# Mixture-of-experts rows kept in DRAM tables by indexed transfers, and one preparatory stage folded into the next

## The chip, the cores and the metric

The kernel runs on one core of one Trainium2 chip. The metric is the time of one execution on the device in microseconds (us); smaller is better.

## The reference, cut to what matters

Two transformer blocks run one after the other on 256 tokens of width 1024 in float32. The first block's second layer ends in a mixture of experts: each token goes to 2 of 8 experts. Then come a final norm and the second block, which needs the spectra of its convolution filters and a memory of 256 rows.

```python
def moe_swiglu(h, router, wg, wu, wd):
    logits = (h @ router).astype(jnp.float32)
    top_v, top_i = lax.top_k(logits, TOP_K)
    gates = jax.nn.softmax(top_v, axis=-1)
    combine = jnp.sum(jax.nn.one_hot(top_i, N_EXPERTS, dtype=jnp.float32) * gates[..., None], axis=-2)
    y = jnp.zeros(h.shape, jnp.float32)
    for e in range(N_EXPERTS):
        y = y + combine[..., e:e + 1] * swiglu(h, wg[e], wu[e], wd[e]).astype(jnp.float32)
    return y.astype(h.dtype)

    # end of first_block, then the filters of second_block
    return rmsnorm(x, final_norm)
    ...
    f = jnp.concatenate([fwd, jnp.zeros((1, HY_ORDER, HY_WIDTH), F32), bwd[1:][::-1]], axis=0)
    f = f / (jnp.sum(jnp.abs(f), axis=0, keepdims=True) + EPS)
    return jnp.fft.rfft(f, axis=0)
```

## The kernel before, in words

The kernel is a fixed sequence of stages; a barrier of the compute engines stands between two of them. SP issues nearly all loads. Weights come in slabs of 1 MB into seven slots (`slots`). For float32 accuracy ScalarE copies a slab to a rounded high part (`w_hi`, and in the experts two more buffers `w_hi_more`, L1241), VectorE subtracts to make the low part (`slots_low`, L1293), and TensorE (PE) multiplies three times per slab: high by high, high by low, low by high.

**Router** (after L2612). PE transposes the gained tokens and scores them; VectorE, in steps that each wait for the one before, finds the two experts of each token, its shares and its rank within each expert (L2694 to L2729). `RC` holds for each pass the rank of every token and its share. `jobs` lists the expert of each pass. The stage's PE program ends with `keep_busy(pe, 14, 4)`, 28 matmuls on zeros.

**Experts** (`experts`, L1057). One pass takes up to 128 tokens of one expert; there are 8 passes, or up to 11 when an expert has more tokens. In the profile there are 8. A pass reads 42 slabs in the order of `plan`: seven groups g of four "first" slabs (gate and up) and two "down" slabs, which come one group later. Within a pass:

- `gather` (L1127) makes the input of the next pass: 16 float32 matmuls multiply the token rows `htm` by a 0/1 selection `sel` (made by `choose`, L1262). PE does it just ahead of the last two down slabs. ScalarE and VectorE then split it to `xh`, `xl` (`source`, L1217 and L1268), after `turned_out` of the last group and ahead of their split of the next pass's first slab.
- `empty` (L1223, L1273) copies the sums of the previous pass from PSUM to `y` at the second slab of a pass.
- `scatter` (L1136) brings `y` of the previous pass back to its tokens: four groups of two float32 matmuls by `back`, placed after slabs 2 to 5 of a pass; VectorE adds each to `res` (`add`, L1277). `back` is made from `marks` (selection times share) by two transposes (`turn_marks`, L1154) and a ScalarE copy (L1248).
- `turn` (L1143) transposes the hidden values of a group, four 128x128 blocks.

SP's loop waits for slab i-7 to be used and then issues slab i (L1107). After the last pass SP fetches six slabs of the next part (L340). The last `empty` and four `scatter`, `add` close the stage. SP goes on past the experts' block only when all engines have left it.

**Opening** (`opening`, L1336 on). SP loads the filter's hidden values, the memory `m_tm`, weights and tables (L2753 to L2773). PE sums the squares of `res`, transposes the memory, and keeps busy (`keep_busy(pe, 40, 1)`); VectorE and ScalarE make the root, split the first slab of layer 0 (`split_hi`, `split_lo`), copy the memory to `memT`, and scale `res` in eight tiles.

**Spectra** (`spectra`, L1441 on). PE first waits for all those loads. Four units i run as a pipeline: PE `make` (L1463), VectorE `window` (L1507), GpSimd clears one row, VectorE `mix` (L1514), PE `transform` (L1477), ScalarE copies the even part, VectorE `join` (L1522), and ScalarE's queue stores the 1 MB result to DRAM. At the start of each unit's `transform` PE does `keep_busy(pe, 8, 4)`. The stage ends when ScalarE has seen all four stores land. Layer 0 of the second block follows.

## Time and profile before

| | us |
|---|---|
| median of 3 runs | 2967.62 (2963.11 to 2969.07) |
| span of the profiled execution, from its first to its last instruction | 2947.1 |
| median of the runs less that span | 20.5 |

The profiled execution's time outside its span is not recorded apart; the runs' median stands 20.5 us above the span, and that is taken for what lies around it. In the profile's rows PE is TensorE's matmuls, PEld its weight loads, DVE VectorE, ACT ScalarE, POOL GpSimd, SPq and ACTq the DMA issues of SyncE and ScalarE. A bracket at the end of a timeline row is the idle time before it and what ended it.

### The profile page before, as it was taken

The page shows a single profiled execution, that of the slowest core. Times are in us where ns is not written, and L with a number is a line of the kernel's source. Part 1 is how long each engine was busy: PE and PEld are TensorE (multiplying, and loading weights), DVE is VectorE, ACT ScalarE, POOL GpSimd, SP SyncE. Part 2 cuts the span into 40 slices and gives each one's busy share as a digit, 9 for nine tenths or more (in the row PEclk, how much of TensorE's full clock was granted, in tenths as well). Part 3 has the DMA queues.
Part 4 walks back from the last instruction along what each step waited for, and adds up shares of the span by engine and source line. Part 5 has one row for each costly group of instructions (what it writes and reads, how often), then busy time and mean ns, then how long its engine had stood idle before and what let it go on. Part 6 is the DMA issues. An engine that isn't in the chain of part 4 may idle for free. (4 is left out here: it accounts for less than half of the span.)

```text
span 2947.1 us, 44951 instructions
## 1 busy us (share of the span) xinstructions
PE 2833.8 (96%) x18499; PEld 2512.2 (85%) x18499; DVE 1999.5 (68%) x1985; ACT 1505.3 (51%) x1445; POOL 66.0 (2%) x56
## 2 busy tenths in 40 slices
PE   7999999899999999999999999999999899999999
PEld 6899998788888888888886778999899788999898
DVE  6555565588888888888885656566555665666554
ACT  3544463476666667666663426444434236444442
POOL 1000000000000000000000210000000100000000
PEclk9999999899999999999999999999999999999999
DMA  6255540699999999999996333454365343444453
GB/s 191 77 188 194 173 158 4 234 367 328 347 347 336 356 329 364 327 350 345 331 361 208 134 103 101 145 171 144 101 199 187 122 128 102 149 140 140 133 190 107
DMA packets 365129, 619.48 MB, mean 210 GB/s; under 512 B 14664, under 2 KB 201126, under 8 KB 363700
## 3 DMA queue, kind: packets, MB, share of 16 engines
q1 hardware_dynamic: 363432, 611.77, 60.8%
q10 hardware_dynamic: 1550, 5.57, 0.5%
q8 instruction: 114, 1.87, 0.3%
q14 instruction: 33, 0.27, 0.0%
HBM read 611.93 MB, written 5.37 MB: 209 GB/s over the span
## 5 line engine op out<-in xcount | busy, mean ns | idle before, releaser
L366 DVE TENSOR_TENSOR slots_low<-slots,w_hi 128x2048 fp32r<-128x2048 f32 x240 | 550.2, 2296 | 372.8 <-ACT w_hi L355 372.5
L355 ACT ACTIVATE w_hi<-slots 128x2048 fp32r<-128x2048 f32 x240 | 452.8, 1891 | 324.7 <-PE ps L949 168.5
L1293 DVE TENSOR_TENSOR slots_low<-slots,w_hi 128x2048 fp32r<-128x2048 f32 x224 | 504.2, 2286 | 68.9 <-ACT w_hi L1241 68.9
L468 PE MATMUL ps<-x_hi,w_hi 128*128 128x256 f32 x1520 | 435.7, 287 | 31.8 <-DVE x_lo_low L553 15.7
L468 PE MATMUL ps<-x_lo_low,w_hi 128*128 128x256 f32 x1520 | 428.9, 282 | 0.0
L468 PE MATMUL ps<-x_hi,slots_low 128*128 128x256 f32 x1520 | 428.7, 282 | 0.0
L1241 ACT ACTIVATE w_hi<-slots 128x2048 fp32r<-128x2048 f32 x224 | 416.9, 1908 | 0.9 <-DMA slots<-in_moe_w_up_dram 0.8
L1173 PE MATMUL ps<-slots_low,x_hi 128*128 128x512 f32 x896 | 352.7, 394 | 0.0
L468 PEld LDWEIGHTS ps<-x_hi,w_hi 128*128 128x128 f32 x1520 | 291.6, 192 | 38.8 <-issue 30.4
L468 PEld LDWEIGHTS ps<-x_lo_low,w_hi 128*128 128x128 f32 x1520 | 291.4, 192 | 0.3
L468 PEld LDWEIGHTS ps<-x_hi,slots_low 128*128 128x128 f32 x1520 | 291.6, 192 | 0.0
L949 PE MATMUL ps<-x_hi,w_hi 128*128 128x256 f32 x960 | 268.2, 279 | 1.0 <-DVE x_lo_low L1015 1.0
L949 PE MATMUL ps<-x_lo_low,w_hi 128*128 128x256 f32 x960 | 266.4, 277 | 0.0
L949 PE MATMUL ps<-x_hi,slots_low 128*128 128x256 f32 x960 | 266.2, 277 | 0.0
L1293 DVE TENSOR_TENSOR slots_low<-slots,w_hi_more 128x2048 fp32r<-128x2048 f32 x112 | 255.2, 2284 | 11.0 <-ACT w_hi_more L1241 11.0
L1173 PE MATMUL ps<-w_hi,x_hi 128*128 128x512 f32 x512 | 206.5, 403 | 12.6 <-DVE slots_low L1293 12.6
L1241 ACT ACTIVATE w_hi_more<-slots 128x2048 fp32r<-128x2048 f32 x112 | 208.7, 1919 | 0.0
L1173 PE MATMUL ps<-w_hi,x_lo_low 128*128 128x512 f32 x512 | 202.1, 395 | 0.0
L1173 PEld LDWEIGHTS ps<-slots_low,x_hi 128*128 128x128 f32 x896 | 169.4, 189 | 36.6
L1232 ACT ACTIVATE hidden_hi<-ps 128x512 fp32r<-128x512 f32 x56 | 33.6, 599 | 293.4 <-PE ps L1143 258.8
L949 PEld LDWEIGHTS ps<-x_hi,w_hi 128*128 128x128 f32 x960 | 180.7, 188 | 2.3 <-issue 1.8
L949 PEld LDWEIGHTS ps<-x_lo_low,w_hi 128*128 128x128 f32 x960 | 180.5, 188 | 0.6
(519 smaller groups left out, 5522.0 us busy)
## 6 DMA issues: line engine op xcount, KB each, us to landing
slots<-in_moe_w_gate_dram SPq DMA_DIRECT2D x112, 1024.0 KB, 5.1
slots<-in_moe_w_up_dram SPq DMA_DIRECT2D x112, 1024.0 KB, 5.1
slots<-in_moe_w_down_dram SPq DMA_DIRECT2D x112, 1024.0 KB, 4.9
slots<-in_mlp_w_dram SPq DMA_DIRECT2D x64, 1024.0 KB, 5.3
slots<-in_w_in_dram SPq DMA_DIRECT2D x54, 1024.0 KB, 5.3
slots<-in_ffn_w_gate_dram SPq DMA_DIRECT2D x14, 1024.0 KB, 5.0
slots<-in_ffn_w_up_dram SPq DMA_DIRECT2D x14, 1024.0 KB, 5.0
slots<-in_ffn_w_down_dram SPq DMA_DIRECT2D x14, 1024.0 KB, 4.9
```

Of the source, the lines that this page charges most:

```text
L355: act.activation(w_hi[:, s.buffer, 0:s.kt * s.cols], slots[:, s.slot, 0:s.kt * s.cols], ACT.Copy).then_inc(w_hi_done, 1)
L366: dve.tensor_tensor(slots_low[:, s.slot, 0:n], slots[:, s.slot, 0:n], w_hi[:, s.buffer, 0:n].bitcast(F32), ALU.subtract).then_inc(w_lo_don ...
L468: mm = pe.matmul(b[:, t * T:(t + 1) * T], w, xx[:, k, :], **flags)
L949: mm = pe.matmul(first_bank(g, n)[:, t * T:(t + 1) * T], ww[:, k, t * P:(t + 1) * P], xx[:, k, :], start=(k == 0 and q == 0), stop=(k == K ...
L1173: mm = pe.matmul(b, xx[:, kx, :], ww[:, k, :], start=(kx == 0 and t == 0), stop=(kx == KD - 1 and t == 2))
L1232: act.activation(hth[:, :], bank(TURN), ACT.Copy).then_inc(turned_hi, 1)
L1241: act.activation(his[i % R], raw[i % NS], ACT.Copy).then_inc(hi_done, 1)
L1293: dve.tensor_tensor(low[i % NS], raw[i % NS], his[i % R].bitcast(F32), ALU.subtract).then_inc(lo_done, 1)
```

## The change

The tables `x_rows` and `y_rows` (12 blocks of 128 rows of 4 KB each) are new in DRAM. The router's stage computes for every token its two places in them (`places`) and no longer the share by pass. SP fills 11 blocks of `x_rows` and 3 of `y_rows` with zeros during the router's first stage. At the start of the experts GpSimd sends every token row to its two places by four indirect transfers of 128 rows. In a pass, right after slab 12, SP stores `y` of the previous pass to `y_rows` and loads the next pass's rows to `xr`; `turn_rows`, eight transposes, takes the place of `gather`, which stays for the first pass. `scatter`, `add`, `marks` and their waits leave the passes. After the last pass SP stores the last `y`, GpSimd waits for it and fetches each token's two rows by four indirect transfers, ScalarE and VectorE weigh and join them, PE transposes, and VectorE adds to `res`.

The `opening` stage is gone: its squares, root, memory transposes, scaling and first split stand inside `spectra`. PE there waits for the first seven loads only (`early`); the others are waited for at the end (`late`). `keep_busy` in `transform` is gone; the wait for the stores moves into layer 0 (a hook of ScalarE). The router's last `keep_busy` is 8 instead of 14.

```diff
+        x_rows, y_rows = (nc.dram_tensor(n, (NJOB, P, D), F32).ap() for n in ("expert_rows_in", "expert_rows_out"))
@@ experts, SP's pass
                             sp.wait_ge(used, SLABS * j + i + 1)
+                            if i == 30:
+                                sp.wait_ge(stored, 16 * j + 16)
...
+                            if i == 12:
+                                sp.wait_ge(rows_sent, 16 * 2 * TT)
+                                sp.wait_ge(act_out, j + 1)
+                                sp.wait_ge(dve_out, j + 1)
+                                sp.dma_start(block_of_rows(y_rows, j), y[:, :]).then_inc(stored, 16)
+                                sp.dma_start(xr[:, :], block_of_rows(x_rows, j + 1)).then_inc(rows_in, 16)
@@ after the passes
                         fetch(sp, after + s)
+                    sp.wait_ge(act_out, n + 1)
+                    sp.wait_ge(dve_out, n + 1)
+                    sp.dma_start(block_of_rows(y_rows, n), y[:, :]).then_inc(stored, 16)
+
+                @block.gpsimd
+                def _(pool):
+                    pool.wait_ge(blanked, 32)
+                    for t in range(TT):
+                        for k in range(2):
+                            pool.indirect_dma_start(x_flat, bass.IndirectOffsetOnAxis(ap=places[:, 0, k, t:t + 1], axis=0), htm[:, t, :], None).then_inc(rows_sent, 16)
+                    n = pool.value_load(jobs[0:1, NJOB:NJOB + 1], min_val=NE, max_val=NJOB - 1)
+                    pool.wait_ge(stored, 16 * n + 16)
+                    pool.tensor_tensor(all_stored[:, :], number[:, 0:1], number[:, 0:1], ALU.add).then_inc(rows_kept, 1)
+                    pool.wait_ge(rows_kept, 1)
+                    for t in range(TT):
+                        for k in range(2):
+                            pool.indirect_dma_start(back[:, t, k, :], None, y_flat, bass.IndirectOffsetOnAxis(ap=places[:, 1, k, t:t + 1], axis=0)).then_inc(back_in[t], 16)
@@ experts, PE
-                    def scatter(j, g):
-                        pe.wait_ge(added, 4 * j + g + 1)
-                        for m in range(2):
-                            f = (2 * g + m) * P
-                            mm = pe.matmul(bank(MISC)[:, m * T:(m + 1) * T], y[:, f:f + P], back[:, :], start=True, stop=True)
-                        mm.then_inc(scattered, 1)
+                    def turn_rows(j):
+                        pe.wait_ge(rows_in, 16 * j + 16)
+                        for half in range(2):
+                            b = bank((GATE, UP)[half][1])
+                            for k in range(4 * half, 4 * half + 4):
+                                mm = pe.transpose(b[:, k % 4 * P:(k % 4 + 1) * P], xr[:, k * P:(k + 1) * P], eye[:, :])
+                            mm.then_inc(gathered, 1)
-                                if (g, n) == (2, 1):
-                                    turn_marks()
-                                if (g, n) in ((0, 3), (1, 0), (1, 1)):
-                                    scatter(j, {(0, 3): 1, (1, 0): 2, (1, 1): 3}[g, n])
                                 if g == G - 1 and n == 0:
-                                    pe.wait_ge(chosen, j + 2)
-                                    gather()
+                                    turn_rows(j)
                     n = passes(pe, body)
-                    for g in range(4):
-                        scatter(n, g)
+                    for t in range(TT):
+                        pe.wait_ge(joined, t + 1)
+                        for k in range(KD):
+                            mm = pe.transpose(bank(2 + k // 2)[:, k % 2 * T + t * P:k % 2 * T + (t + 1) * P], back[:, t, 0, k * P:(k + 1) * P], eye[:, :])
@@ experts, ScalarE and VectorE after the passes
+                        act.activation(back[:, t, 0, :], back[:, t, 0, :], ACT.Copy, scale=gg[:, t, 2:3]).then_inc(weighed, 1)
+                        dve.scalar_tensor_tensor(out=back[:, t, 0, :], in0=back[:, t, 1, :], scalar=gg[:, t, 3:4], in1=back[:, t, 0, :],
+                                                 op0=ALU.mult, op1=ALU.add).then_inc(joined, 1)
-                        add(n, g)
+                        dve.tensor_tensor(flat(res[:, 2 * g:2 * g + 2, :]), flat(res[:, 2 * g:2 * g + 2, :]), bank(2 + g), ALU.add)
@@ router
+                    nc.sync.dma_start(x_rows.rearrange("a p n -> p a n")[:, 1:NJOB, :], blank[:, :].unsqueeze(1).broadcast_to([P, NJOB - 1, D])).then_inc(blanked, 16)
+                    nc.sync.dma_start(y_rows.rearrange("a p n -> p a n")[:, NE + 1:NJOB, :], blank[:, :].unsqueeze(1).broadcast_to([P, NJOB - 1 - NE, D])).then_inc(blanked, 16)
-                            keep_busy(pe, 14, 4)
+                            keep_busy(pe, 8, 4)
@@ spectra, PE
-                                keep_busy(pe, 8, 4)
+                                else:
+                                    pe.wait_ge(memory_act_out, 2)
+                                    pe.wait_ge(memory_dve_out, 2)
-                        pe.wait_ge(*needs)
+                        mean_squares()
+                        pe.wait_ge(*early)
                         make(0)
+                        turn_memory()
@@ spectra, VectorE
                         window(0)
                         mix(0)
+                        for g in (1, 3):
+                            dve.wait_ge(memory_turned, g + 1)
+                            dve.tensor_copy(flat(memT[:, 2 * g:2 * g + 2, :]), bank(4 + g)).then_inc(memory_dve_out, 1)
+                        dve.reciprocal(ms[:, :], ms[:, :]).then_inc(root_inverted, 1)
                         for i in range(N):
                             if i + 1 < N:
                                 window(i + 1)
+                            else:
+                                split_lo(dve, BEFORE_MOE, len(stream.slabs))
...
                             join(i, 1)
+                            scale_tiles(range(3 * i, min(3 * i + 3, KD)))
@@ spectra, ScalarE
-                        act.wait_ge(spectra_out, 16 * N)
```

## Rows read from the trace of the kernel before

**Rows 1.** The page's first line.
```profile
span 2947.1 us, 44951 instructions
```
**Rows 2.** Busy time by stretch: one pass, the opening, the spectra.
```profile
core 0: us, PE busy (x) PEld busy (x) DVE busy (x) ACT busy (x) POOL busy (x), PEclk, DMA share, GB/s
810.90:939.00 128.10, 127.46 (x582) 104.33 (x582) 107.39 (x68) 88.18 (x64) 0.00 (x0) 1.00 0.96 343
...
1587.50:1608.60 21.10, 17.98 (x125) 15.27 (x125) 8.68 (x13) 6.48 (x7) 1.46 (x2) 0.84 0.70 204
1608.60:1658.00 49.40, 46.57 (x220) 29.00 (x220) 30.13 (x46) 12.79 (x16) 11.54 (x8) 0.97 0.27 107
```
**Rows 3.** Waits in six passes, 690 to 1446 us: total, times, longest.
```profile
PEld ps L1173 <- DVE slots_low L1293: 5.6, 5, 1.1
```
**Rows 4.** DMA, 540 to 560 us, in 40 slices; last column issue to landing.
```profile
GB/s 0 0 0 0 0 53 111 254 389 406 401 414 406 410 397 393 393 377 389 389 389 389 385 381 385 393 385 385 385 389 389 393 406 365 365 393 397 393 385 381
...
slots<-in_moe_w_gate_dram SPq DMA_DIRECT2D x4, 1024.0 KB, 10.9
```
**Rows 5.** DMA, 690 to 1446 us: packets, MB, share; issues to landing.
```profile
q1 hardware_dynamic: 109972, 261.12, 96.5%
...
slots<-in_moe_w_gate_dram SPq DMA_DIRECT2D x83, 1024.0 KB, 5.1
```
**Rows 6.** DMA issues of the whole span: KB each, median us to landing.
```profile
m_tm<-in_mem_dram SPq DMA_DIRECT2D x1, 1024.0 KB, 5.6
...
out_dram<-rows_out ACTq DMA_DIRECT2D x2, 512.0 KB, 2.7
```
**Rows 7.** Timeline of a pass's end and the next one's start.
```profile
797.47 0.59 PEld L1143 LDWEIGHTS ps<-eye,hidden 128*128 128x128 f32 x4
...
800.70 3.77 PEld L1127 LDWEIGHTS ps<-select,by_token 128*128 128x128 f32 x32
...
804.40 0.30 PEld L1195 LDWEIGHTS ps<-w_hi_more,hidden_hi 128*128 128x128 f32 x2
...
806.62 3.72 ACT L1241 ACTIVATE w_hi<-slots 128x2048 fp32r<-128x2048 f32 x2
...
808.56 4.49 DVE L1293 TENSOR_TENSOR slots_low<-slots,w_hi 128x2048 fp32r<-128x2048 f32 x2 [2.53 <-ACT w_hi L1241]
...
810.91 0.19 PEld L1173 LDWEIGHTS ps<-w_hi,x_hi 128*128 128x128 f32 x1 [1.11 <-DVE slots_low L1293]
...
819.05 0.86 PEld L1136 LDWEIGHTS ps<-select_back,y 128*128 128x128 f32 x4
...
819.93 0.19 PEld L1173 LDWEIGHTS ps<-w_hi,x_hi 128*128 128x128 f32 x1
```
**Rows 8.** Line L1154: ns min/median/max, first and last start.
```profile
L1154 PEld LDWEIGHTS ps<-eye,share_marks x16: 140/142/142, 589.5 to 1486.4; 128*128 128x128 f32 x16
```
**Rows 9.** Timeline from the router's end to the first expert load.
```profile
531.02 6.02 PE L630 MATMUL ps<-zeros 128*128 128x256 bf16 x28
...
533.03 0.16 DVE L2729 CAST passes<-passes_f 1x13 int32<-1x13 f32 x1
...
541.67 1.04 SPq L1107 DMA_DIRECT2D slots<-in_moe_w_gate_dram  x2
```
**Rows 10.** Timeline of the experts' end.
```profile
1579.06 0.60 ACT L1223 ACTIVATE y<-ps 128x512 f32<-128x512 f32 x1 [5.05 <-PE ps L1195]
...
1586.76 0.69 DVE L1277 TENSOR_TENSOR res<-res,ps 128x512 f32<-128x512 f32 x1 [1.22 <-PE ps L1136]
1587.72 0.53 SPq L2753 DMA_DIRECT2D filter_hidden<-filter_hidden  x1
```
**Rows 11.** Timeline of the opening's end and the spectra's start.
```profile
1602.11 1.75 DVE L1373 RECIPROCAL mean_square<-mean_square 128x256 f32<-128x256 f32 x1
...
1608.59 7.11 PE L1463 MATMUL ps<-hy_w,filter_hidden 65*128 65x512 f32 x16 [0.97 <-PEq L181]
...
1615.54 1.91 PE L630 MATMUL ps<-zeros 128*128 128x256 bf16 x16
```

More of the change, by code:

```diff
@@ L1057, in experts @@
         def experts(gate, up, down, routed, after):
-            RC, htm, jobs, row_number, number, before, over = routed
+            rank, htm, jobs, row_number, number, before, over, gg, places = routed
             W, G, NS, R, KH = 512, 7, 7, 6, 4
@@ L1295, in body @@
                                 empty(j)
-                            if (kind, g) == ("first", 1):
-                                add(j, n)
                             if (kind, n) == ("first", 0) and g >= 1:
@@ L1439, in sine_layers, with spectra @@
             return {("act", 0): tables, ("pe", 0): first, ("dve", 1): angle(0), ("act", 2): sine(0), ("pe", 2): second, ("dve", 3): angle(1), ("act", 4): store}
-        def spectra(h2, w3s, needs):
+        def spectra(h2, w3s, tiles, m_tm, early, late):
+            gain = gain_of("final_norm", 0)
             dft = K["dft"][:, :].rearrange("p (t s k) -> p t s k", t=TT, s=2)
@@ L1445, in spectra @@
             with ExitStack() as c:
-                fb = sb(c, "filters", [P, 2, TT, 512])
-                pq = [sb(c, "combined", [P, 2, TT, 512]) for _ in range(2)]
-                ab = sb(c, "sizes", [P, 2, TT, 512])
-                F = sb(c, "spectra", [P, 4, 512])
+                fb, pq, ab, ms = tiles
+                F = m_tm[:, :, :].rearrange("p t (a n) -> p (t a) n", n=512)
                 evens = flat(x_lo_plain[:, 0:4, :]).rearrange("p (s n) -> p s n", s=2)
@@ L1452, in spectra, with mean_squares, turn_memory @@
                 N = len(U)
-                with stage("made", "windowed", "lag0", "mixed", "absd", "added", "summed", "sized", "inverted", "transformed", "evens_out", "joined") as \
-                        (block, made, windowed, lag0, mixed, absd, added, summed, sized, inverted, transformed, evens_out, joined):
+                sq = x_hi_plain
+                with stage("made", "windowed", "lag0", "mixed", "absd", "added", "summed", "sized", "inverted", "transformed", "evens_out", "joined",
+                           "ones_row", "squared", "means_made", "shifted", "rooted", "root_inverted", "scaled", "memory_turned", "memory_act_out", "memory_dve_out") as \
+                        (block, made, windowed, lag0, mixed, absd, added, summed, sized, inverted, transformed, evens_out, joined,
+                         ones_row, squared, means_made, shifted, rooted, root_inverted, scaled, memory_turned, memory_act_out, memory_dve_out):
                     @block.tensor
                     def _(pe):
+                        def mean_squares():
+                            for h in range(2):
+                                pe.wait_ge(squared, h + 1)
+                                for k in range(4 * h, 4 * h + 4):
+                                    mm = pe.matmul(bank(7)[:, 0:T], ones[:, :], sq[:, k, :], start=(k == 0), stop=(k == KD - 1))
+                            mm.then_inc(means_made, 1)
+                        def turn_memory():
+                            pe.wait_ge(memory_in, 16)
+                            for g in range(KD // 2):
+                                if g == 3:
+                                    pe.wait_ge(shifted, 1)
+                                for kk in range(2):
+                                    for t in range(TT):
+                                        k = 2 * g + kk
+                                        mm = pe.transpose(bank(4 + g)[:, kk * T + t * P:kk * T + (t + 1) * P], m_tm[:, t, k * P:(k + 1) * P], eye[:, :])
+                                mm.then_inc(memory_turned, 1)
                         def make(i):
@@ L1499, in _, with scale_tiles @@
                     def _(dve):
+                        def scale_tiles(tiles):
+                            for k in tiles:
+                                dve.scalar_tensor_tensor(out=res[:, k, :], in0=res[:, k, :], scalar=gain(k), in1=ms[:, :], op0=ALU.mult, op1=ALU.mult).then_inc(scaled, 1)
                         def window(i):
@@ L2740, in program @@
                 by_row = [A[n][0].rearrange("e (k p) n -> p e k n", p=P) for n in ("moe_w_gate", "moe_w_up", "moe_w_down")]
-                experts(*by_row, (RC, htm, jobs, row_number, number, before, over), BEFORE_MOE)
+                experts(*by_row, (rank, htm, jobs, row_number, number, before, over, gg, places), BEFORE_MOE)
         memT = sb(ctx, "memory", [P, KD, T])
@@ L2776, in program @@
                 fetch(sp, i)
-            with stage("cleared_") as (block, cleared_):
-                @block.gpsimd
-                def _(pool):
-                    pool.memset(wlr_all[:, :, :, :], 0.0).then_inc(cleared, 1)
-                    pool.memset(h2[64:65, :, :], 1.0)
-            opening(m_tm)
-            cm.close()
-            spectra(h2, w3s, (spectra_in, 16 * loads))
+            spectra(h2, w3s, (fb, pq, ab, ms), m_tm, early, (tables_in, 16 * loads))
         for l in range(2):
```

199 lines of the change are left out of this document (88 added, 111 removed).

## The prediction

> **What bounds the kernel now.** I read the page first, for the span [rows 1], then the busy time by stretch. In a pass of the experts PE is busy 127.46 of 128.10 us, VectorE 107.39, ScalarE 88.18, and the DMA engines show a share of 0.96 [rows 2]. A pass lasts 128.1 us by a line that runs once in each: (1486.4 - 589.5) / 7 [rows 8]. So eight passes hold a third of the time, and the question is which of two full resources sets their pace. Two views decide it. In the waits of six passes PE stands still for VectorE's low part five times, 1.1 us each [rows 3], and for nothing else. And a slab lands 5.1 us after its issue in these six passes [rows 5]; at the start, when six or more slabs are queued, it takes 10.9 [rows 4]. In the passes no queue builds up: SP issues a slab when PE has freed a slot, and the DMA follows. So PE's own instructions set the pace, and what is taken off PE in a pass shortens it, as far as the DMA and VectorE can follow.
>
> **The change part by part, in a pass.** Scatter goes: its four matmul instructions hold the weight-load queue from 819.05 to 819.93, 0.88 us, four times a pass [rows 7]: 3.5 us. The two transposes of the marks go: at 0.59 / 4 = 0.15 each [rows 7] 0.3 us. Gather held it from 800.70 to 804.40, 3.70 us [rows 7]; eight transposes at 0.15 take its place, 1.2 us, so 2.5 us less. Not all of that arrives. The stall of 1.11 us at the next pass's first matmul hangs on a chain: gather, ScalarE's two copies, its split of the next first slab at 806.62, VectorE's low part at 808.56 [rows 7]. With the transposes both copies are ready as soon as ScalarE has the last group's hidden values; I place the split 2.3 us earlier, so the pass gains 2.3 and the stall grows a little. Together 3.5 + 0.3 + 2.3 = 6.1 us. The scatters also gave VectorE time: slabs 2 to 5 each had 0.88 us more. In slabs 4 to 7 I follow PE at 2.75 us a slab and VectorE at 4.49 / 2 = 2.25 [rows 7] with its two other operations, and find margins of 0.1 to 0.5 us; four adds of 0.69 [rows 10] leave VectorE too. I take 0.5 off: **5.6 us a pass**, 122.5 us. VectorE has then some 104.6 us of work in 122.5.
>
> What is added to a pass is on the DMA: 0.5 MB stored and 0.5 MB loaded behind slab 12, one slab more than 42. SP's waits there ask for copies made at the pass's second slab, and its wait at slab 30 is for a store issued eighteen slabs before; behind them stand only loads that are not yet due. 43 slabs are 45.1 MB; in 122.5 us that is 368 GB/s. With a queue standing the trace shows 377 to 397 GB/s in most half microseconds and 385 or 389 in the steady ones [rows 4]; at 389 the 45.1 MB take 116 us. So I cost the added rows at nothing: they come when five loaded slabs wait in the slots, and a landing of 5.1 us may grow by 2.7 there. If that cover were gone, they would cost 2.7 us a pass. The bounds for the seven later passes are a gain of 2 us each (the DMA rival below) and 6.1 each.
>
> The Trainium skill, SBUF — State Buffer, section "A bandwidth-pool intuition that's wrong (but worth ruling out)", gives HBM to one core as about 358 GB/s and calls HBM almost always the end-to-end bottleneck. The trace shows more, 385 to 389 GB/s held with a queue. By the page's figure a pass would take 126 us, an estimate, and the whole some 2952 us.
>
> Seven passes: 7 x 5.6 = **39.2 us less**.
>
> **First pass.** The same 5.6 us less, but GpSimd's four indirect transfers write 2 MB about when the first slabs load, with a queue standing [rows 4]. At 389 GB/s that is 5.4 us of DMA time. Between 0 (all done before the first load) and 5.4 I take 2.5, since they can begin some 3 us before the first load. **3.1 us less.**
>
> **Router.** Its end is PE's keep-busy: 28 matmuls of 6.02 us from 531.02, to 537.0; VectorE has finished at 533.2 [rows 9]. Sixteen take 3.4 us: 2.6 us less. VectorE loses eight small steps and gets twelve, at 0.2 us each (its last one took 0.16 [rows 9]), and ends near 534.0, still before. `pick_more` loses three steps of 0.25, and SP's first load at 541.67 [rows 9] waits for it: 0.7 us. The blank rows are 14 stores of 0.5 MB, 7.3 MB, 19 us at 389 GB/s, issued near 514 on an idle DMA; done near 534, ahead of the first load. **3.3 us less**; nothing, if they run late.
>
> **End of the experts.** This grows. Before, from `y` copied (1579.06 + 0.60) to the last add (1586.76 + 0.69) it took 7.8 us [rows 10]. After: the store of `y`, as the 512 KB of the output, 2.7 [rows 6], and 0.2 to hand over; GpSimd's small add 0.5; four indirect transfers; ScalarE's weighing, two of its 0.60 copies, 1.2; VectorE's join, two of 0.69, 1.4; eight transposes at twice 0.15 after the pause, 2.4; four adds, 2.8. No row shows an indirect transfer. Below: four overlapped 512 KB moves, 2.7 + 3 x 1.35 = 6.7. Above: one after another, each as the 1 MB memory load, 5.6 [rows 6], 22.4. I take 9, near the lower end, as they move 4 KB rows like the output's store, with 2.3 more for GpSimd to make 512 addresses. Sum 20.2, so **12.4 us more** (10 to 26).
>
> The Trainium skill, DMA: Bandwidth & Descriptors, section "Anatomy of one DMA — SWDGE (gpsimd) path", fits such a transfer as 2.0 us plus the bytes at 436 GB/s: 3.2 us for 512 KB, an estimate. One after another they would take 12.8 us in place of my 9, and the whole 2932 us. No row here shows one.
>
> SP's next loads began at 1587.72, 0.3 us after the last add, though SP had been idle [rows 10]: they wait for the block's end and move with it.
>
> **Opening and spectra.** Before, the first spectra matmul starts 1608.59 - 1587.72 = 20.9 us after the first load's issue [rows 10, 11]. The DMA engines are busy 0.70 x 21.1 = 14.8 us there for 4.3 MB [rows 2]; the seven early loads and the memory are 3.3 MB of it, 11.3 us, and with some 2.7 for the first to land [rows 6] PE can start at 14: 6.9 us earlier. PE has paused before, so I let the first unit's matmuls, 7.11 / 2 = 3.55 us [rows 11], run half their time at half clock: 1.8 back. VectorE's reciprocal, 1.75 [rows 11], and two copies of 0.69 now stand ahead of the second window: 3.1 back. That leaves 2.0. The keep-busy of 1.91 us [rows 11] goes from three units in which PE is the pace (busy 46.57 of 49.40 [rows 2]); VectorE gets 1.2 us of scaling in each and I count 1.4 for each unit, 4.3. The split of layer 0's first slab takes the place of a window in the last unit, where VectorE waits for a store. **6.3 us less** (0 to 11).
>
> **The sum.** -39.2 - 3.1 - 3.3 + 12.4 - 6.3 = -39.5 us. The profiled span of 2947.1 [rows 1] becomes 2908; the runs' median, 20.5 us above it, becomes **2928 us**. Two of the six high buffers move in memory, as the tiles ahead of them change size; I cost that at nothing, and allow 1 us a pass either way.
>
> **The rivals.** (a) The DMA sets the pass. For it: share 0.96 now at 261.12 MB in 756 us, 345 GB/s; divided by the 96.5% of [rows 5] that is 358 GB/s, so 45.1 MB need 126 us, 2 us less a pass and not 5.6. Against it: landings stay at 5.1 us. Time: 3.5 x 7 = 25 us of the gain is lost, 2952. The page's 358 is the same case. (b) VectorE's low part becomes late in every group. For it: the thin margins above. Against: 104.6 of 122.5 us. At 0.4 us for each of seven groups, 2.8 us a pass, 22 over all: 2950. (c) Slower than before: GpSimd's indirect transfers are slow because it makes 128 row addresses for each. Place: the experts' end, where all engines wait. With t for one, the end costs 4t in place of 9. The gain of 39.5 is gone at t = 12.1 us, 95 ns a row; at 16 us the time is 2983. From about that point the rows sent ahead of the first pass are late for SP's wait at slab 12 as well. For it: nothing on GpSimd in the trace tells its price. Against: each row is 4 KB, and 128 are few.
>
> **How the numbers follow.** The forecast 0.60, with its own range 2915 to 2941; (a) 0.13; (b) 0.10; (c), any indirect transfer over 6 us, 0.17, of which 0.06 stays faster. A change within 0.2%, 6 us, can't be told from none. Faster 0.60 + 0.13 + 0.10 + 0.06 = 0.89, rounded to 0.88; same 0.05; slower 0.07. The range for 8 in 10 goes from 2913, where the bounds fall well together (passes 6.1, the first one undisturbed, the end 10, the spectra 11: 14 us), to 2954, which takes in (a) and (b).
>
> **What would show it.** Passes of 122 to 123 us with PE as busy as now and slabs landing in under 8 us: the main term. Landings that grow to 10 us and more, with PE waiting on low parts that wait on loads: (a). Waits of PE on VectorE of 0.3 us or more in each group at usual landings: (b). At the experts' end: last matmul to next loads about 21 us; more than 30 is (c). First spectra matmul about 14 us after the loads' start, units of 9 and not 10.4 us. The prediction is wrong above all if the passes stay over 126 us.

## The result, and the profile after

The changed kernel takes 2917.35 us (median of 4 runs, 2916.47 to 2919.49), the kernel before on the same chip 2965.86 (4 runs, 2963.11 to 2969.07): 0.9848 of it, 95% interval 0.9822 to 0.9874. The prediction was 2928, range 2913 to 2954, faster.

Every later listing gives an execution's own time beside its span; the time is the span and 1.75 to 1.9 us (once 2.3). The profile of before was thus one of some 2949 us, and the 20.5 us between the runs' median and the span of [rows 1] do not lie around the span. By the profiles the change is worth 31 us, by the runs 48. Profiled and timed executions of the kernel before differ in TensorE's mean granted clock: 0.987 in the profile, 0.979 to 0.984 in most timed ones (below, first experiment). So stages are compared by profile, whole kernels by runs. One run of `spectra_busy` below, 3509.96 us at a mean clock of 0.742, is left out of its median.

The page's first line of the changed kernel, the busy time of one pass (columns as in [rows 2]), the waits and the DMA of six passes, and the line that stores a pass's result, which runs once in each pass:

```profile
span 2915.9 us, 43813 instructions
```
```profile
904.20:1026.00 121.80, 121.01 (x542) 98.32 (x541) 104.05 (x60) 87.86 (x62) 0.00 (x0) 1.00 1.01 371
```
```profile
PE ps L1217 <- DVE hidden_lo L1305: 4.9, 6, 1.0
...
PEld ps L1200 <- DVE slots_low L1311: 1.9, 6, 0.3
```
```profile
slots<-in_moe_w_up_dram SPq DMA_DIRECT2D x86, 1024.0 KB, 5.3
...
expert_rows_out<-y SPq DMA_DIRECT2D x6, 512.0 KB, 6.7
next_rows<-expert_rows_in SPq DMA_DIRECT2D x6, 512.0 KB, 7.4
```
```profile
L1124 SPq DMA_DIRECT2D expert_rows_out<-y x8: 367/368/1081, 575.2 to 1428.1; - x8
```

A pass lasts (1428.1 - 575.2) / 7 = 121.8 us where it lasted 128.1 [rows 8]. PE is as busy in it as before [rows 2], the stall on the low part that was 1.1 us in five of six passes [rows 3] is 0.3, and the wait has gone to the last group's hidden values, 4.9 / 6 = 0.8 us. Slabs land in 5.3 us; right behind the added rows, at slab 13, a landing takes 8.6 us (median of six passes), and it is back at 5.2 by slab 30.

The end of the experts, the counterpart of [rows 10], from the timeline:

```profile
1531.92 0.60 ACT L1245 ACTIVATE y<-ps 128x512 f32<-128x512 f32 x1 [5.77 <-PE ps L1217]
...
1532.83 0.36 SPq L1134 DMA_DIRECT2D expert_rows_out<-y  x1
1535.67 0.19 POOL L1144 TENSOR_TENSOR all_stored<-number 128x1 f32<-128x1 f32 x1 [991.29 <-DMA expert_rows_out<-y]
1536.14 0.98 POOL L1148 DMA_INDIRECT rows_back<-expert_rows_out,places  x1 [0.27 <-POOL all_stored L1144]
1537.42 0.95 POOL L1148 DMA_INDIRECT rows_back<-expert_rows_out,places  x1 [0.30 <-issue]
...
1542.91 1.15 ACT L1277 ACTIVATE rows_back<-rows_back,shares 128x1024 f32<-128x1024 f32 x1 [10.39 <-DMA rows_back<-expert_rows_out,places]
...
1545.46 1.15 ACT L1277 ACTIVATE rows_back<-rows_back,shares 128x1024 f32<-128x1024 f32 x1 [1.40 <-DMA rows_back<-expert_rows_out,places]
...
1549.99 2.48 DVE L1345 TENSOR_TENSOR res<-res,ps 128x512 f32<-128x512 f32 x4 [2.06 <-PE ps L1232]
1552.73 0.53 SPq L2784 DMA_DIRECT2D filter_hidden<-filter_hidden  x1
```

The store of `y` takes 2.8 us, GpSimd hands over an indirect transfer every 1.25 us, and the second pair has landed 9.3 us after the first transfer was issued (1536.14 to 1545.46).

The spectra stage in tens of us, the changed kernel first, then the kernel of the first experiment that has this change's experts and the old opening and spectra (clock: third number from the end):

```profile
1566.60:1576.60 10.00, 10.00 (x23) 5.76 (x24) 4.25 (x6) 0.83 (x2) 0.52 (x1) 0.50 0.15 56
1576.60:1586.60 10.00, 10.00 (x38) 5.74 (x37) 9.97 (x13) 4.16 (x6) 2.87 (x2) 0.97 0.01 2
1586.60:1596.60 10.00, 10.00 (x21) 4.17 (x19) 8.58 (x13) 2.49 (x4) 3.03 (x2) 0.66 0.55 210
```
```profile
1575.30:1585.30 10.00, 10.00 (x36) 5.28 (x37) 7.62 (x10) 2.25 (x3) 2.95 (x2) 1.00 0.00 0
1585.30:1595.30 10.00, 10.00 (x49) 6.19 (x48) 7.31 (x11) 2.95 (x4) 3.38 (x3) 1.00 0.26 107
1595.30:1605.30 10.00, 10.00 (x49) 6.19 (x48) 7.31 (x11) 3.20 (x4) 2.87 (x2) 1.00 0.55 210
```

PE is busy throughout in both, but in the changed kernel it runs at 1.2 GHz, half clock, in all of the first stretch and in two thirds of the third (0.50 and 0.66). The first unit's eight matmuls take 7.19 us where 16 took 7.11 before [rows 11], after PE has waited 5.94 us for loads, and the memory's transposes take 3.62:

```profile
1566.58 7.19 PE L1439 MATMUL ps<-hy_w,filter_hidden 65*128 65x512 f32 x8 [5.94 <-DMA dft<-in_c_dft_dram]
...
1573.57 3.62 PE L1430 MATMUL ps<-eye,m_tm 128*128 128x128 f32 x16
```

And VectorE's scaling, beside GpSimd's add, in the same stage:

```profile
1587.42 3.35 DVE L1484 SCALAR_TENSOR_TENSOR res<-res,vectors,mean_square 128x256 f32<-128x256 f32 x3
...
1587.98 2.52 POOL L1550 TENSOR_TENSOR sizes<-sizes 128x1024 f32<-128x1024 f32 x1 [4.56 <-ACT sizes L1560]
...
1590.70 0.15 DVE L1536 TENSOR_SCALAR filter_size<-ps 128x4 f32<-128x4 f32 x1
...
1590.92 0.50 PEld L1455 LDWEIGHTS ps<-combined,dft 128*128 128x128 f32 x2 [1.38 <-issue]
```

The three tiles take 3.35 us. The line's own durations (shortest, median, longest, in ns) say how:

```profile
L1484 DVE SCALAR_TENSOR_TENSOR res<-res,vectors,mean_square x8: 467/474/2617, 1587.4 to 1610.2; 128x256 f32<-128x256 f32 x8
```

A tile takes 0.47 us, but the one that comes up while GpSimd adds ends only after the add, and takes 2.6 us. The filter's size (L1536) stands behind it, and PE's next transform behind the size.

Stage by stage, in us of the two profiles:

| stretch | before | after | difference | predicted |
|---|---|---|---|---|
| start to the router's squares (same code) | 512.9 | 515.6 | +2.7 | 0 |
| router, to the first expert load | 28.8 | 27.0 | -1.8 | -3.3 |
| first load to the experts' last matmul | 1037.3 | 989.3 | -48.0 | -42.3 |
| to the spectra's loads | 8.8 | 20.8 | +12.1 | +12.4 |
| to the first spectra matmul | 20.9 | 13.9 | -7.0 | -6.9 |
| to layer 0's first matmul | 50.6 | 56.0 | +5.4 | +0.6 |
| to the end (same code) | 1287.9 | 1293.3 | +5.4 | 0 |

The stages that the change touches sum to -39.3 us. The two that it does not touch add 8.1; over the 14 profiles of this study the first of them takes 512.9 to 526.7 us, the last 1283.6 to 1293.4.

### The profile page after: what moved, and what is told of

It is laid out like the page before. It is cut to its first block and busy times, and to the rows that moved or that the text cites. A ratio compares the mean times of both kernels' runs of the same rounds, so it can differ in the third digit from the quotient of the medians.

```text
span 2915.9 us, 43813 instructions
## 1 busy us (share of the span) xinstructions
PE 2779.7 (95%) x17995; PEld 2459.6 (84%) x17995; DVE 1980.1 (68%) x1922; ACT 1506.8 (52%) x1439; POOL 75.1 (3%) x66
## 5 line engine op out<-in xcount | busy, mean ns | idle before, releaser
L471 PE MATMUL ps<-x_hi_low,w_hi 128*128 128x256 f32 x1520 | 435.9, 287 | 32.9 <-DVE x_lo_low L556 15.3
L471 PE MATMUL ps<-x_hi_low,slots_low 128*128 128x256 f32 x1520 | 428.8, 282 | 0.0
L1200 PE MATMUL ps<-slots_low,x_hi_low 128*128 128x512 f32 x896 | 351.6, 392 | 0.0
L471 PEld LDWEIGHTS ps<-x_hi_low,w_hi 128*128 128x128 f32 x1520 | 292.6, 192 | 39.9 <-issue 30.6
L471 PEld LDWEIGHTS ps<-x_hi_low,slots_low 128*128 128x128 f32 x1520 | 292.8, 193 | 0.0
L952 PE MATMUL ps<-x_hi_low,w_hi 128*128 128x256 f32 x960 | 269.0, 280 | 1.0 <-DVE x_lo_low L1018 1.0
L952 PE MATMUL ps<-x_hi_low,slots_low 128*128 128x256 f32 x960 | 267.0, 278 | 0.0
L1200 PE MATMUL ps<-w_hi,x_hi_low 128*128 128x512 f32 x512 | 203.7, 398 | 9.1 <-DVE slots_low L1311 9.1
L1200 PEld LDWEIGHTS ps<-slots_low,x_hi_low 128*128 128x128 f32 x896 | 168.9, 189 | 36.9
L952 PEld LDWEIGHTS ps<-x_hi_low,w_hi 128*128 128x128 f32 x960 | 180.6, 188 | 2.3 <-issue 1.8
L952 PEld LDWEIGHTS ps<-x_hi_low,slots_low 128*128 128x128 f32 x960 | 181.4, 189 | 0.0
```

The lines of the kernel that those rows point to most:

```text
L471: mm = pe.matmul(b[:, t * T:(t + 1) * T], w, xx[:, k, :], **flags)
L952: mm = pe.matmul(first_bank(g, n)[:, t * T:(t + 1) * T], ww[:, k, t * P:(t + 1) * P], xx[:, k, :], start=(k == 0 and q == 0), stop=(k == K ...
L1200: mm = pe.matmul(b, xx[:, kx, :], ww[:, k, :], start=(kx == 0 and t == 0), stop=(kx == KD - 1 and t == 2))
```

## The experiments

Each ran beside the kernel before; a ratio is to that. They ran on four chips, on which the kernel before took 2955.8 to 2965.8 us (medians), so times of two rows compare to some us only. Medians of 5 runs unless said.

**The two parts apart, and the kernel before once more.** `experts_only` is before with the tables alone, `spectra_only` before with the merged opening and spectra alone; `before_again` is before.

> The experts by tables alone; opening, memory's transposes and spectra stage as before. Theory: this part carries the whole gain. By the two traces the passes gave 48.0 us (6.4 a pass and 3.2 in the first), the router 1.8, and the experts' end took 12.0 back: 37.8 us less, about 2928 us against 2966 of before. Rival: the merged spectra stage is worth ten us or more of the 48.5 that the runs differ by; then this kernel stays above 2932. In the profile: passes of 121.7 to 122 us, last matmul of the experts to next loads 20 to 21 us, loads to first spectra matmul 20.9 us as before.

> The merge of opening and spectra alone; experts as before. Theory: the first spectra matmul comes 7 us earlier after the loads and the stretch from it to layer 0's first matmul takes 56 us where it took 50.6, so 1.6 us less in all: 2964 against 2966, not to be told from no change. Rival: it is worth the 10 us that the runs leave beside the experts' part: 2956.

> The kernel before, unchanged, for a second profile. Its first profiled execution took 2949 us, its timed runs 2958 to 2971, while the profiles of every other kernel lie within 10 us of their timed runs. Theory: the first profile caught an execution with a quick first block (its router stage began at 512.9 us; the others' at 515.6 to 521.5, with the same code up to there), and a second profile will show a span of 2955 to 2970 with the excess before the router stage or in the two last layers, not in the experts. Rival: profiled executions of this kernel are always some 17 us quicker than timed ones; then this one shows 2945 to 2950 again.

| kernel | runs, us | ratio (95%) | passes | last matmul to loads | to spectra | to layer 0 |
|---|---|---|---|---|---|---|
| `experts_only` | 2919.30 | 0.9852 (0.9829 to 0.9875) | 121.8 | 21.4 | 20.6 | 50.4 |
| `spectra_only` (6 runs) | 2951.85 | 0.9954 (0.9938 to 0.9970) | 127.9 | 11.4 | 15.0 | 56.2 |
| `before_again` (11 runs) | 2966.57 | 1.0022 (1.0005 to 1.0039) | 128.1 | 8.8 | 21.1 | 50.4 |

The kernel before, run against itself, comes out at 1.0022 with an interval that leaves out 1: differences of some 0.2%, 6 us, are not to be read.

The experts' tables alone give the changed kernel's time within its interval; on top of them the merge takes another 2 us off, nothing that the runs can tell. They come out 9 us under their forecast of 2928. Alone on the kernel before, the merge measured 14 us less where 2 were forecast, though its own stretches, from the experts' last matmul to layer 0, are 2.2 us longer than before's in the profiles: by their rows it gains nothing, and where the 14 us are stays open. The two parts' gains, 46 and 14 us, are not additive either: the whole measured 48.5. The second profile of before is again of an execution at a high clock:

```profile
core 0: 2944.4 us, clock 0.986
```

Of the 57 runs of before in these experiments, the 11 at a mean clock of 0.986 to 0.988 took 2945 to 2958 us, the 45 at 0.979 to 0.984 took 2958 to 2977 (one at 0.985: 2956). So the theory of a second profile at 2955 us and more fell, and the 17 us go with the clock. That is a correlation: no profile of the kernel before at 0.98 was caught, so in which stage the 17 us lie stays open. The rival on record, that a profiled execution of this kernel is always quicker, is not excluded: both profiles are of quick ones, and one run in five is.

**Terms of the pass, put back.** Two kernels restore PE's old work in the passes of the changed kernel, `scatter_back` and `gather_back`; a third, `rows_4mb`, adds DMA. Their edits, in that order:

```diff
+    def scatter(g):
+        for m in range(2):
+            f = (2 * g + m) * P
+            pe.matmul(bank(MISC)[:, m * T:(m + 1) * T], y[:, f:f + P], htm[:, 0, 0:T], start=True, stop=True)
...
+    if g == 0 and n == 2:
+        pe.wait_ge(act_out, j + 1)
+        pe.wait_ge(dve_out, j + 1)
+        scatter(0)
+    if (g, n) in ((0, 3), (1, 0), (1, 1)):
+        scatter({(0, 3): 1, (1, 0): 2, (1, 1): 3}[g, n])
```
```diff
-    turn_rows(j)
+    pe.wait_ge(rows_in, 16 * j + 16)
+    gather()
```
```diff
+    EXTRA = (13, 16, 19, 22, 28, 31, 34)
...
+    if i in EXTRA:
+        m = EXTRA.index(i)
...
+        sp.dma_start(back[:, m % 4 // 2, m % 2, :], block_of_rows(x_rows, j + 1)).then_inc(extra_in[m], 16)
```

> The changed kernel with the scatter's matmul instructions put back into each pass, two at each of slabs 2 to 5, their results left unused and no adds behind them. Theory: PE sets the pass, so the four times 0.88 us of the prediction come back, 3.5 us: passes of 125.2 us where there are 121.7, some 28 us over eight passes. Rival: VectorE or the DMA sets the pass by now; then there is slack for them on PE and the passes stay under 123.

> The changed kernel with the old gather's sixteen matmul instructions at the end of each pass in place of the eight transposes; they fetch pass 0's rows every time, so every pass computes on those. Theory: the end of the pass hangs on the chain of gather, copies and the next first slab's split, so 2.3 us come back, up to the 2.5 that gather takes longer: passes of 124.0 to 124.3 us. Rival: the chain has slack and the passes stay under 122.5; then the gain of 6.4 a pass came from the scatter and VectorE's adds.

> The changed kernel with seven more loads of 0.5 MB in each pass (the next pass's rows again, to where nothing reads them before the experts' end): 45.1 + 3.7 = 48.8 MB a pass. Theory: PE sets the pass and the DMA has the rate that a standing queue showed, 385 to 389 GB/s, so the pass grows only to 48.8 MB / 389 = 125.4 us, 3.7 more, with landings that no longer fall back to 5 us: about 30 us in all. Rival: at 45.1 MB in 121.7 us, 370 GB/s, the DMA is at its end already; then the passes take 131.9 us and the run 80 us more. If it can do more than 389, the passes stay under 124.

The store's line in each, once a pass, in that order:

```profile
L1124 SPq DMA_DIRECT2D expert_rows_out<-y x8: 367/368/393, 578.8 to 1455.2; - x8
```
```profile
L1124 SPq DMA_DIRECT2D expert_rows_out<-y x8: 367/368/1177, 577.9 to 1447.5; - x8
```
```profile
L1129 SPq DMA_DIRECT2D expert_rows_out<-y x8: 368/368/903, 576.9 to 1450.6; - x8
```

Passes of 125.2, 124.2 and 124.8 us against 121.8; by their one run each the kernels take 2944.69, 2937.61 and 2937.35 us. The scatter costs 3.4 us (predicted 3.5), gather 2.4 in place of the transposes (2.3), so PE's instructions set the pass. The marks' two transposes (0.3 by their rows) were not put back. With 3.7 MB more a pass grows by 3.0 us, where the DMA, if it were at its end at 370 GB/s would have made it 131.9. The DMA and the waits of six passes of `rows_4mb`:

```profile
DMA packets 117633, 288.93 MB, mean 393 GB/s; under 512 B 4844, under 2 KB 4844, under 8 KB 117631
...
slots<-in_moe_w_gate_dram SPq DMA_DIRECT2D x84, 1024.0 KB, 11.7
```
```profile
ACT w_hi_more L1273 <- DMA slots<-in_moe_w_gate_dram: 53.0, 46, 2.0
```

Landings stay at 12 us, ScalarE waits for slabs, and 393 GB/s is what the DMA gives here. The changed kernel's 371 GB/s is near that: by this estimate the DMA would set the pass once some 121.8 x (1 - 371 / 393) = 6.8 us more were taken off PE.

**What the experts' end costs.** The indirect fetches are replaced by plain loads on SP's queue.

```diff
-    pool.indirect_dma_start(back[:, t, k, :], None, y_flat, bass.IndirectOffsetOnAxis(ap=places[:, 1, k, t:t + 1], axis=0)).then_inc(back_in[t], 16)
+    sp.dma_start(back[:, t, k, :], y_rows[2 * t + k]).then_inc(back_in[t], 16)
```

GpSimd's small add ahead of its transfers goes with them.

> The changed kernel with the experts' results fetched by four plain loads of 512 KB on SP's queue in place of GpSimd's four indirect ones; they fetch the first four tables as they stand, so tokens get rows that are not theirs. It prices the indirection. The four indirect transfers took 9.3 us from the first issue to the first weighing, of which GpSimd's own steps of 1.25 us are 5. Theory: the transfer of 2 MB sets most of it, 5.4 us at 389 GB/s and some 2 us for the first to land, so plain loads save 1.5 to 2.5 us, and last matmul to next loads falls from 20.8 to 18.5. Rival: the making of addresses sets it; then plain loads take 4 us less and the end 16 to 17 us.

```profile
1542.72 1.77 SPq L1138 DMA_DIRECT2D rows_back<-expert_rows_out  x4
1547.56 1.15 ACT L1274 ACTIVATE rows_back<-rows_back,shares 128x1024 f32<-128x1024 f32 x1 [7.89 <-DMA rows_back<-expert_rows_out]
...
1551.25 1.15 ACT L1274 ACTIVATE rows_back<-rows_back,shares 128x1024 f32<-128x1024 f32 x1 [2.54 <-DMA rows_back<-expert_rows_out]
```

The last pair lands 8.5 us after the first issue in place of 9.3, and last matmul to next loads takes 19.5 us; it takes 20.8 in the changed kernel and 21.1 to 21.6 in five others with indirect fetches and no added loads. The indirection, GpSimd's small add included, is worth 1 to 2 us; the rest is 2 MB on their way and the chain behind them.

**What the merged spectra stage loses.** `scale_moved` moves the scaling, `spectra_busy` puts keep-busy matmuls back.

```diff
     window(i + 1)
...
+    if i:
+        scale_tiles(range(3 * i - 3, min(3 * i, KD)))
     join(i, 0)
...
     join(i, 1)
-    scale_tiles(range(3 * i, min(3 * i + 3, KD)))
```
```diff
     mean_squares()
+    keep_busy(pe, 20, 4)
     pe.wait_ge(*early)
...
     if s == t == 0:
...
+        keep_busy(pe, 8, 4)
```

> The changed kernel, with the scaling of res three, three and two tiles at a time behind the window products of units 1 to 3, and the size added up right behind the joins. Theory: in the changed kernel the scaling stalls while GpSimd adds the sizes (3.35 and 3.40 us for three tiles that take 1.2 alone) and PE waits behind it for the size. Away from that add, three tiles take 1.2 to 1.3 us, the transforms of units 1 and 2 begin 1 and 2 us earlier, and the stretch from the first spectra matmul to layer 0's first matmul falls from 56.0 to about 52.5 us; the run comes out 3 to 4 us under the changed kernel's 2917. Rival: the units are paced by matmuls at half clock; then the stretch stays at 55 to 56 us whatever VectorE does.

> The changed kernel with keep-busy matmuls in the spectra stage: twenty pairs while PE waits for the loads, and the old eight pairs ahead of each unit's first transform. Theory: what the merge lost lies in the granted clock. With the old keep-busy work it was 1.00 for the first thirty us of the spectra (0.50, 0.97 and 0.66 in those of the changed kernel); with it back the first unit's eight matmuls take 3.6 and not 7.2 us, the transposes 1.9 and not 3.6, units 1 and 3 transform in 3.6 and not 5.3; against it stand 1.9 us for each unit, half of it in waits that PE has there anyway. From the first spectra matmul to layer 0's first: 56.0 falls to 47 to 50, the run to about 2909. Rival: the scaling behind GpSimd's adds sets the units and the clock is a symptom of PE's waits; then the stretch stays at 56 or grows by the 1.9 us of some units.

`scale_moved`: 2911.75 us, ratio 0.9821 (0.9802 to 0.9840). Of its timeline:

```profile
1595.54 2.34 POOL L1551 TENSOR_TENSOR sizes<-sizes 128x1024 f32<-128x1024 f32 x1 [3.75 <-ACT sizes L1561]
...
1599.32 6.09 PE L1455 MATMUL ps<-combined,dft 128*128 128x512 f32 x8
...
1600.17 1.27 DVE L1484 SCALAR_TENSOR_TENSOR res<-res,vectors,mean_square 128x256 f32<-128x256 f32 x3
```

Three tiles take 1.27 us alone, and no tile of this kernel more than 0.48:

```profile
L1484 DVE SCALAR_TENSOR_TENSOR res<-res,vectors,mean_square x8: 472/476/479, 1600.2 to 1622.8; 128x256 f32<-128x256 f32 x8
```

That the scaling waits for the add is shown. What it costs the stage is not: the stretch to layer 0 came to 54.6 us where 52.5 was forecast, and the five kernels with unaltered spectra code (the changed kernel, `scatter_back`, `gather_back`, `rows_4mb`, `plain_tail`) take 54.2 to 56.6. The transform of unit 1, 5.29 us in the changed kernel, took 6.09 here at half clock, and the matmuls before it 6.33 in place of 5.47, so part of what the move gave went to the clock. The profiled execution, 2922.95 us, is the slowest of this kernel's five.

`spectra_busy`: 2920.02 us, ratio 0.9863 (0.9834 to 0.9892); the stretch grew to 60.9 us where 47 to 50 was forecast. Its clock in tens of us, its first unit's matmuls and one of its keep-busy groups:

```profile
1573.00:1583.00 10.00, 10.00 (x49) 6.07 (x48) 8.63 (x11) 3.08 (x4) 2.86 (x2) 1.00 0.06 19
1583.00:1593.00 10.00, 10.00 (x32) 5.23 (x31) 10.00 (x15) 3.20 (x4) 2.98 (x2) 0.78 0.26 106
1593.00:1603.00 10.00, 10.00 (x41) 5.93 (x39) 5.20 (x8) 1.19 (x2) 0.52 (x1) 0.71 0.29 105
```
```profile
1572.05 3.71 PE L1439 MATMUL ps<-hy_w,filter_hidden 65*128 65x512 f32 x8 [1.99 <-DMA dft<-in_c_dft_dram]
...
1593.79 3.62 PE L633 MATMUL ps<-zeros 128*128 128x256 bf16 x16
```

The first unit is cured: its eight matmuls take 3.71 us, not 7.19. The keep-busy work inside the units did not hold the clock, and it stands on the path: it waits for the size too, behind the scaling, and 1.9 us become 3.6 at half clock. So here keep-busy work cured the unit behind PE's wait for loads, and cost time ahead of the transforms.

**Taking the experts' end back.** The spectra's loads need nothing of the experts' result. `early_loads` issues them inside the experts' end, to space that is free there; `combined` adds the moved scaling, loads ahead of the last six slabs, window products ahead of the mean square on VectorE, and keep-busy matmuls on PE where it waits for rows. In all three PE sums the squares of `res` behind the first unit's matmuls and no longer ahead of them. `combined_2` loads the transform table and the first weights ahead of the first pass. The edit of `combined`, where part 0 is the transform table, the first filter weights and the hidden values, part 1 the window, part 2 the memory and the second filter weights (in `early_loads` part 0 stands behind the six fetches):

```diff
     n = passes(sp, body)
+    ahead(sp, 0)
     for s in range(AHEAD):
...
     sp.dma_start(block_of_rows(y_rows, n), y[:, :]).then_inc(stored, 16)
+    sp.wait_ge(stored, 16 * n + 16)
+    ahead(sp, 1)
+    for t in range(TT):
+        sp.wait_ge(back_in[t], 32)
+    ahead(sp, 2)
...
     pe.wait_ge(src_lo_done, 2 * n + 2)
+    keep_busy(pe, 40, MISC)
```

> The changed kernel, with what the spectra stage loads issued inside the experts' last 20 us: the transform table, the first filter weights and the hidden values before y is stored, the window behind its store, the memory and the second filter weights behind the fetched rows. Theory: the 13.9 us between the loads and the first spectra matmul are transfer time that needs nothing of the experts' result; hidden there, the first spectra matmul follows the last add of the experts within 2 to 3 us, and the run falls by 9 to 11 us to about 2907. Rival one: the loads slow the four indirect transfers, the experts' end grows by 3 to 5 us and the gain is 5 to 7. Rival two: PE is slow after the pause whatever is loaded, the stretch behind the first spectra matmul grows by as much as is won, and the run stays at 2917.

> The changed kernel with what the runs so far point to: the scaling away from GpSimd's add; the spectra's loads inside the experts' end, now ahead of the last six slabs' fetches so that y's store has no queue before it; the first window products ahead of the mean square on VectorE; keep-busy matmuls on PE in the experts' end (40 pairs behind the last matmul, 12 behind the transposes). Theory: the experts' end stays at 21 to 22 us, the first spectra matmul follows the last add by 2 us, at full clock, and from the experts' last matmul to layer 0's first it takes 75 to 80 us where the changed kernel took 90.7; the run comes to 2902 to 2908. Rival: PE falls to half clock later in the stretch instead, as with the keep-busy work in the spectra stage, and what the loads give is given back: 85 us and more, 2912 to 2917.

> The combined kernel with the transform table and the first filter weights loaded ahead of the first pass and the hidden values behind y's store, so that the last slabs' fetches have the queue to themselves. Theory: y's store took 6.1 us in the combined kernel and 2.8 in the changed one because 1.7 MB more stood in the queue ahead of it; with 2.8 again, last matmul to the spectra's first matmul falls from 26.5 to about 23 us, the run by 3 us to about 2902. Rival: the store waits for the six slabs that are fetched there in any case, and its 6.1 us stay; then nothing changes.

| kernel | runs, us | ratio (95%) | last matmul to first spectra matmul | to layer 0 |
|---|---|---|---|---|
| changed kernel | 2917.35 | 0.9848 (0.9822 to 0.9874) | 34.7 | 56.0 |
| `early_loads` | 2915.91 | 0.9829 (0.9810 to 0.9848) | 28.1 | 61.3 |
| `combined` | 2905.34 | 0.9804 (0.9785 to 0.9823) | 26.5 | 50.3 |
| `combined_2` | 2905.77 | 0.9819 (0.9788 to 0.9850) | 24.3 | 50.3 |

`early_loads` missed its forecast of 2907. The store of `y` had a queue before it, 8.7 us where it took 2.8, and VectorE's window products waited behind the mean square, which by the edit now came late. The clock was 0.51 in the first 10 us of its spectra, as the forecast's second rival has it:

```profile
1538.81 0.38 SPq L1136 DMA_DIRECT2D expert_rows_out<-y  x1
...
1547.47 0.19 POOL L1151 TENSOR_TENSOR all_stored<-number 128x1 f32<-128x1 f32 x1 [996.88 <-DMA expert_rows_out<-y]
...
1577.92 0.42 DVE L1525 TENSOR_SCALAR mean_square<-ps 128x256 f32<-128x256 f32 x1 [12.91 <-PE ps L1426]
```

In `combined` the first spectra matmuls follow the experts' last add by 2.0 us and run at 2.4 GHz; the granted clock is 1.00 over the stage's first 20 us:

```profile
1545.90 0.37 SPq L1136 DMA_DIRECT2D expert_rows_out<-y  x1
1552.10 0.19 POOL L1151 TENSOR_TENSOR all_stored<-number 128x1 f32<-128x1 f32 x1 [995.05 <-DMA expert_rows_out<-y]
...
1571.42 3.68 PE L1450 MATMUL ps<-hy_w_early,filter_hidden_early 65*128 65x512 f32 x8 [0.92 <-POOL filter_hidden_early L1556]
```

From last matmul to layer 0 it takes 76.8 us where the changed kernel takes 90.7, as forecast; the runs fell by 12.0, on another chip. Several things were changed together, so which of them gave what is not shown. `combined_2` brings the store to 3.8 us, 2.1 us less at the end, and loses at the start, where first load to first matmul took 14.9 in place of 12.0 us, of which 1.4 us are left at the experts' last matmul. The forecast gain of 3 us did not come: its runs can't be told from those of `combined`.

## Why the prediction was right, point by point

- **What bounds the passes** was right: PE's instructions, with VectorE and DMA behind them. Rival (a), the DMA, would have shown 131.9 us for 48.8 MB; it was 124.8. Of the Trainium skill's 358 GB/s (SBUF — State Buffer, section "A bandwidth-pool intuition that's wrong (but worth ruling out)") the runs show more: 371 in the passes, 393 under load. Rival (b) did not come: VectorE's stall fell to 0.3 us a pass.
- **A pass** was 5.6 us by the sum and is 6.3. Scatter 3.5 (3.4 by experiment) and gather 2.3 (2.4) were right; the 0.5 taken off for VectorE's thin margins was not needed. Seven passes gave 44.0 us, not 39.2.
- **The first pass** was 3.1 and is 48.0 - 44.0 = 4.0 less.
- **Router**: 3.3 forecast, 1.8 by the profiles; with the changed router the other kernels show 26.5 to 28.6 us and `spectra_only`, with the old one, 27.2. It can't be told from nothing.
- **Experts' end**: +12.4 forecast, +12.1. The choice of 9 us for the indirect transfers, near the lower bound, is 9.3; rival (c) needed 12.1 for each of the four. By the Trainium skill's fit for one such transfer (DMA: Bandwidth & Descriptors, section "Anatomy of one DMA — SWDGE (gpsimd) path") four that waited for each other would take 12.8, an estimate. Issued 1.25 us apart, the four had landed in 9.3, so they overlap.
- **Opening**: the first spectra matmul came 13.9 us after the loads' start, forecast 14.
- **Spectra** is the step that failed: 0.6 us more was the sum, 5.4 it is (3.6 to 6.0 over the five profiles with this code), and the transforms of the units begin 10.1 us apart, not 9. Two terms were wrong. The half clock was sized at 1.8 us, half of the first unit's matmuls. All of them ran at it (+3.6), and so did the memory's transposes (3.62 us against 1.91 in `spectra_busy`) and two thirds of the stage's third ten us. And the scaling of three tiles was taken as 1.2 us in time that VectorE has free; it is 3.35 beside GpSimd's add, ahead of the size that PE waits for. How the miss divides between the two stays open: with the scaling moved alone the stage takes 54.6 us, inside the unaltered code's spread. With the scaling moved and the clock at 1.00 for 20 us, in `combined`, it takes 50.3, as long as before, but there the loads and the order on PE and VectorE differ too.
- **The sum** of the touched stages is -39.3 against a forecast of -39.5. That it is so close is luck: the passes gave 5.7 more than forecast, the spectra lost 4.8 more, and the router 1.5. The base was wrong, too. 20.5 us between span and runs were carried over as fixed, where 1.8 lie there: 18.7 too many. The code that did not change took 8.1 us more in this profile. The two leave the runs 10.7 us under the forecast of 2928. So the time was met within its range partly by luck: a base too high and unchanged code that took longer stood against each other. Why the runs gained 48.5 us where the rows of the touched stages show 39.3 stays open: the profile of before is of an execution some 17 us quicker than its median run, and no slower one was profiled.

## What to carry to other kernels

Where one engine sets a loop's pace, count its own instructions: scatter and gather, put back one by one, each cost within 0.1 us what their rows had said. A merge of two stages is to be priced by what stands beside each operation as well: here the scaling beside GpSimd's add, and matmuls behind a pause of PE, took more than their rows had said. And when a chain of transfers is added at a stage's end, look what of the next stage's loads needs nothing of it. Issued early by themselves these loads gave nothing that the runs can tell (2915.91 against 2917.35); with the scaling moved, the window products first and PE kept busy through the wait, 12 us. And take a forecast's base from runs whose own span is known: two executions of one kernel differed by 32 us here.

## What the runs showed of the hardware

- A VectorE operation with two inputs in SBUF, the core's on-chip memory, was held up beside a GpSimd add: a tile's scaling that takes 0.47 us took 2.6 when it came up during the add. A subtraction of two SBUF inputs in the changed kernel, of the form that takes 2.28 to 2.30 us in the passes of before, took 2.80 where its first 0.64 us fell into such an add. VectorE's reciprocal, one input, took 1.74 beside such an add and 1.75 without [rows 11]. The Trainium skill, SBUF — State Buffer, section "Who interferes with whom", says this: two SBUF inputs on VectorE contend with a GpSimd instruction that reads SBUF, and one input, outside VectorE's two-port modes, does not. The trace agrees on both.

```profile
1578.59 1.74 DVE L1523 RECIPROCAL mean_square<-mean_square 128x256 f32<-128x256 f32 x1
1578.94 2.35 POOL L1550 TENSOR_TENSOR sizes<-sizes 128x1024 f32<-128x1024 f32 x1 [3.86 <-ACT sizes L1560]
...
1610.46 2.40 POOL L1550 TENSOR_TENSOR sizes<-sizes 128x1024 f32<-128x1024 f32 x1 [4.69 <-ACT sizes L1560]
1612.22 2.80 DVE L369 TENSOR_TENSOR slots_low<-slots,w_hi 128x2048 fp32r<-128x2048 f32 x1 [1.49 <-ACT w_hi L358]
```

- The granted clock fell to 0.66 in a stretch in which PE was busy 10.00 of 10.00 us with 32-bit matmuls, and to 0.71 where keep-busy matmuls stood among them; with the old order of the stage it held 1.00 for thirty us. What of the order decides it, these runs do not tell.
- The DMA engines held 393 GB/s over six passes, 289 MB.
